# Odd blocks of routed rows transposed by VectorE from quarter-row gathers, even ones by TensorE, and gate and up weights loaded in 8 KB pieces

## What is computed

```python
def body(acc, blk):
    toks, bw, e = blk                      # 128 rows of the table, their weights, one expert
    xb = hp[toks]                          # gather
    yb = (jax.nn.silu(xb @ w_gate[e]) * (xb @ w_up[e])) @ w_down[e]
    return acc.at[toks].add(yb.astype(f32) * bw[:, None]), None
```

## Time and profile before

| | |
|---|---|
| median of three runs | 2494.95 us |
| profiled execution | 2485.66 us |
| its span, first to last instruction | 2483.8 us |
| granted TensorE clock, mean over the span | 0.985 |
| TensorE busy | 2382.5 us (96%) |
| VectorE busy | 1575.5 us (63%) |
| ScalarE busy | 1161.9 us (47%) |
| GpSimd busy | 767.3 us (31%) |
| HBM traffic over the span | 211 GB/s |

### The profile page before, as it was taken

The page is one execution under the profiler, slowest core; times in us unless marked ns, Lnnn a source line. Parts: engine busy times, 40 slices in busy tenths (PEclk is TensorE's granted clock), DMA queues, the critical chain, the costliest instruction groups (busy, mean ns, idle before and its releaser), DMA issues. The chain is left out here.

```text
span 2483.8 us, 49979 instructions
## 1 busy us (share of the span) xinstructions
PE 2382.5 (96%) x11840; PEld 1954.7 (79%) x11842; DVE 1575.5 (63%) x2285; ACT 1161.9 (47%) x1621; POOL 767.3 (31%) x829
## 2 busy tenths in 40 slices
PE   8899999989997799999999999999999999999986
PEld 6677777678886688888888888888888888888875
DVE  6686867768878756555665555656665556655447
ACT  4525253542225645445554445545554445544334
POOL 0010100011110134334543433534443334444327
PEclk9999999989998899999999999999999999999998
DMA  7242323364445579778988878888888789987863
GB/s 254 77 144 98 111 94 111 117 218 164 171 164 206 196 230 284 223 219 270 273 259 233 254 218 263 268 266 262 257 253 243 224 223 274 283 247 222 216 221 136
DMA packets 253808, 524.34 MB, mean 211 GB/s; under 512 B 18065, under 2 KB 165169, under 8 KB 249649
## 3 DMA queue, kind: packets, MB, share of 16 engines
q1 hardware_dynamic: 204464, 336.64, 39.7%
q0 software_dynamic: 48672, 186.86, 29.4%
q10 hardware_dynamic: 608, 0.02, 0.0%
HBM read 386.61 MB, written 136.87 MB: 211 GB/s over the span
## 5 line engine op out<-in xcount | busy, mean ns | idle before, releaser
L2503 PE MATMUL psG<-gu_split,xT_hi 128*128 x2624 | 624.3, 390 | 2.9 <-ACT xT_hi L2340 1.5
L2503 PEld LDWEIGHTS psG<-gu_split,xT_hi 128*128 128x128 f32 x2624 | 493.8, 188 | 106.2 <-issue 3.6
L2326 POOL DMA_INDIRECT acc<-y,si x162 | 290.1, 1791 | 728.6 <-DMA acc<-y,si 413.3
L2409 DVE TENSOR_TENSOR gu_split<-raw_gu,gu_split (+1 forms) x127 | 290.6, 2288 | 175.3 <-ACT gu_split L2344 171.7
L2514 PE MATMUL psG<-gu_split,xT_lo 128*128 x1304 | 339.3, 402 | 5.9 <-issue 5.8
L2514 PEld LDWEIGHTS psG<-gu_split,xT_lo 128*128 128x128 f32 x1304 | 233.1, 188 | 50.1 <-issue 8.7
L2344 ACT ACTIVATE gu_split<-raw_gu x126 | 234.3, 1907 | 33.5 <-issue 33.5
L2301 POOL DMA_INDIRECT xg<-htab,gi x164 | 205.0, 1250 | 130.4 <-POOL gi L2298 109.7
L2409 DVE TENSOR_TENSOR d_lo<-raw_d,d_hi (+1 forms) x64 | 146.7, 2292 | 149.5 <-ACT d_hi L2344 149.5
L2389 ACT ACTIVATE HT_hi<-psH 128x256 fp32r<-128x256 f32 x162 | 62.4, 385 | 351.6 <-PE psH L2521 351.6
L2406 DVE TENSOR_TENSOR xT_lo<-psX,xT_hi 128x512 fp32r<-128x512 f32 x328 | 209.7, 680 | 8.5 <-ACT xT_hi L2340 8.5
(11 more groups left out here) (388 smaller groups left out, 3723.7 us busy)
## 6 DMA issues: line engine op xcount, KB each, us to landing
raw_gu<-in_w_gate_dram SPq DMA_DIRECT2D x64, 1024.0 KB, 6.0
raw_gu<-in_w_up_dram SPq DMA_DIRECT2D x64, 1024.0 KB
raw_d<-in_w_down_dram SPq DMA_DIRECT2D x64, 1024.0 KB, 6.9
wring<-split_d SPq DMA_DIRECT2D x24, 1024.0 KB, 4.8
split_d<-wring POOLq DMA_DIRECT2D x8, 1024.0 KB, 4.2
raw_d<-mixed SPq DMA_DIRECT2D x16, 512.0 KB, 3.9
xt<-in_x_dram SPq DMA_DIRECT2D x16, 512.0 KB, 4.3
htab<-h SPq DMA_DIRECT2D x16, 512.0 KB, 2.6
```

Source lines behind the costliest of these rows:

```text
L2326: nc.gpsimd.indirect_dma_start(out=acc, out_offset=bass.IndirectOffsetOnAxis(ap=si[k][:, 0:1], axis=0), in_=y[k][:], in_offset=None, compu ...
L2409: nc.vector.tensor_tensor(dst, src, hi, ALU.subtract).then_inc(dlo_s if n == 2 else gulo_s, 1)
L2503: nc.tensor.matmul(psG[slot][:], xT_hi[slot][:, c, :], right[:, bass.ds(w, 1), c, :].rearrange("p a n -> p (a n)"), start=(n == 0 and c == ...
```

## The change

A second DRAM table `hcut` holds each token's row in four quarters, each of 256 features and 16 expert weights (1088 bytes). `output_and_route` stores each tile there too (`store_h`: one more DMA of 512 KB per tile; `store_weights`: one more DMA per tile in pieces of 64 bytes), and the zero rows get four more DMAs. `indices()` gains 16 small VectorE operations that write `pidx`, the quarter-row numbers of odd blocks.

In the loop, an odd block is gathered by four indirect DMAs of 128 quarter rows each, so that partition group a (32 partitions) holds quarter a of all 128 rows. VectorE turns it with its 32x32 block transpose: one operation over 1024 elements per partition into `xF`, and one over 128 for the weights. TensorE then only transposes the 128x128 piece with the weights into `psW`. ScalarE and VectorE form `xT_hi` and `xT_lo` of an odd block in one operation each, from SBUF. Even blocks are still transposed by TensorE, now reading every eighth feature.

Gate and up weights land with partition p holding rows 8p to 8p+7, contiguous, 8 KB each, gate and up apart; the split pieces are gate and up in place of the two halves of k. Every eighth feature of a row is the order that goes with it. The index copies `gi` and `si` of the loop move from GpSimd to ScalarE.

```diff
+def gather_pieces(nc, hcut, to, at, done):
+    for g in range(QUADS):
+        nc.gpsimd.indirect_dma_start(out=to[:, g, 0:PIECE], out_offset=None, in_=hcut.rearrange("r a w -> (r a) w"),
+                                     in_offset=bass.IndirectOffsetOnAxis(ap=at[:, g:g + 1], axis=0)).then_inc(done, 16)
...
+                dve.wait_ge(idx_s, 2)
+                odd = idx[:].rearrange("p (b k) -> p b k", k=2)[:, :, 1]
+                for a in range(QUADS):
+                    for g in range(QUADS):
+                        last = nc.vector.tensor_scalar(pidx[a * QP:(a + 1) * QP, :, g], odd[g * QP:(g + 1) * QP], float(QUADS), float(a),
+                                                       ALU.mult, ALU.add)
...
+def runs_view(raw_gu):
+    return raw_gu[:].rearrange("p s k n -> p s (k n)").rearrange("p s (h k n) -> p s h k n", h=2, n=FE)
...
-                        sp.dma_start(dst, w[0, bass.ds(e, 1)].rearrange("a (k p) n -> p (a k) n", p=P)).then_inc(sm, 16)
+                        rows = "a (k p) n -> p (a k) n" if sm is down_in else "a (p k) n -> p (a k) n"
...
 GpSimd, body of the loop
-                    pool.wait_ge(turned[1], s.n + 3)
-                    pool.wait_ge(pairw_s, s.n + 3)
+                    pool.wait_ge(next_gi_s, s.n + 1)
+                    if k == 0:
+                        pool.wait_ge(pairw_s[0], s.turn + 2)
                     carry_wait(pool, passed)
-                    gather(s.n + AHEAD, k, s.n + AHEAD + 1)
-                    nc.gpsimd.tensor_copy(si[k][:], idx[:, bass.ds(s.n, 1)]).then_inc(si_s, 1)
+                    if k:
+                        gather_pieces(nc, hcut, xg[1], gi[1], x_in[1])
+                    else:
+                        gather_rows(nc, htab, xg[0], gi[0], x_in[0])
...
 ScalarE, body of the loop
-                    evac_x(s.n + 3, k)
+                    high_x(s.turn + 2, k)
+                    gather_index(s, k)
                     silu(s.n + 2, 1 - k, s.n + 1)
                     when_first(act, nexts[n + 1], lambda: split_gate_up(nexts[n + 1], s.n + 2))
                     s.wait(act, yps_s[0])
-                    act.wait_ge(added[k], s.turn * 16)
+                    scatter_index(s, k)
...
 VectorE
+            def turn_x(nth):
+                dve.wait_ge(x_in[1], nth * 16 * QUADS)
...
+                nc.vector.transpose(xF[:, 0:KC, :].rearrange("p c (g j) -> p c g j", g=QUADS),
+                                    xg[1][:, :, 0:FEATS].rearrange("p g (i c) -> p c g i", c=KC))
+                nc.vector.transpose(xF[:, KC, :].rearrange("p (g j) -> p g j", g=QUADS),
+                                    xg[1][:, :, FEATS:WIDE]).then_inc(odd_turned, 1)
...
+                    low_x(s.turn + 2, k)
                     s.wait(dve, H_s)
-                    pair_weight(nexts[n + 1], k, s.turn + 2)
-                    product(s.n + 2, 1 - k)
+                    if k == 0:
+                        pair_weight(nexts[n + 1], s.turn + 2, 0)
+                        pair_weight(nexts[n], s.turn + 1, 1)
+                    product(s.n + 2, 1 - k, s.turn + 1 + k)
+                    if k == 0:
+                        turn_x(s.turn + 2)
...
 TensorE
+                rows = xg[0][:, 0:D].rearrange("p (q c) -> p c q", c=KC)
...
+                        m = nc.tensor.transpose(psX[h][:, c, :], rows[:, h * HALF + c], ident[:])
...
-                    pe.wait_ge(x_in[1 - k], (s.turn + k + 2) * 16 )
-                    carry_wait(pe, passed)
-                    for h in range(2):
-                        pe.wait_ge(xlo_s[h], s.n + 3)
-                        turn_x(1 - k, h)
+                    if k:
+                        turn_weights(s.turn + 2)
+                        turn_x(s.turn + 3)
```

More of the change, by code:

```diff
@@ L2128, in _, with load_expert, experts @@
                     down(n)
-def load_expert(eng, w_gate, w_up, w_down, expert, slot, wgu, wd, loaded):
-    for w, sm, dst in zip((w_gate, w_up, w_down), loaded, (wgu[:, slot, :, 0:FE], wgu[:, slot, :, FE:], wd[:, slot])):
-        eng.dma_start(dst, w[0, expert].rearrange("(k p) n -> p k n", p=P)).then_inc(sm, 16)
-def experts(nc, passed, w_gate, w_up, w_down, ident, htab, acc, table, n_turns, idx, xg, gi, gi_s, x_in, acc_out, gu, guhi_s, gulo_s, wgu, wd, loaded, y, si, added,
+def load_expert(eng, w_gate, w_up, w_down, expert, slot, wgu, wd, loaded, by_run=False):
+    gate, up = (runs_view(wgu)[:, slot, h] for h in range(2)) if by_run else (wgu[:, slot, :, 0:FE], wgu[:, slot, :, FE:])
+    for w, sm, dst in zip((w_gate, w_up, w_down), loaded, (gate, up, wd[:, slot])):
+        rows = "(p k) n -> p k n" if by_run and w is not w_down else "(k p) n -> p k n"
+        eng.dma_start(dst, w[0, expert].rearrange(rows, p=P)).then_inc(sm, 16)
+def experts(nc, passed, w_gate, w_up, w_down, ident, htab, hcut, acc, table, n_turns, idx, pidx, tails_s, xg, gi, gi_s, x_in, acc_out, gu, guhi_s, gulo_s, wgu, wd, loaded, y, si, added,
             prefetch_shared, prefetch_hT):
@@ L2175, in experts @@
         xlo_s = [sem(f"xlo_s{i}") for i in range(2)]
-        pairw_s = sem("pairw_s")
+        odd_turned = sem("odd_turned")
+        odd_wturn = sem("odd_wturn")
+        odd_xhi = sem("odd_xhi")
+        odd_xlo = sem("odd_xlo")
+        next_gi_s = sem("next_gi_s")
+        pairw_s = [sem(f"pairw_s{i}") for i in range(2)]
         dhi_s = sem("dhi_s")
@@ L2206, in expert, with column @@
                 return within(self.word & (EXPERTS - 1), 0, EXPERTS - 1)
+            def column(self):
+                share = EXPERTS // QUADS
+                return within((self.word & (EXPERTS - 1)) + (self.word & (EXPERTS - share)), 0, P - 1)
             def next(self):
@@ L2446, in _ @@
             split_first(1)
[L2447 to L2448 removed]
+            low_x(1, 0)
             split_first(2)
[L2450 to L2451 removed]
+            for k in range(2):
+                dve.wait_ge(acc_out[k], 16 * EARLY // 2)
+            pair_weight(block0, 1, 0)
+            dve.wait_ge(tails_s, 1)
+            turn_x(1)
             when_first(dve, block0, lambda: split(block0, 0))
[L2453 to L2455 removed]
+            product(1, 0, 1)
+            low_x(1, 1)
             when_first(dve, block0, lambda: split(block0, 1))
@@ L2483, in _, with turn_x, turn_weights, gate_up_high @@
         def _(pe):
-            def turn_x(slot, half):
-                for c in range(HALF):
-                    m = nc.tensor.transpose(psX[half][:, c, :], xg[slot][:, (half * HALF + c) * P:(half * HALF + c + 1) * P], ident[:])
-                m.then_inc(turned[half], 1)
-            def gate_up_high(nth, slot, entry):
-                for h in range(2):
-                    pe.wait_ge(xhi_s[h], nth)
+            def turn_x(nth):
+                pe.wait_ge(x_in[0], nth * 16)
+                carry_wait(pe, passed)
+                rows = xg[0][:, 0:D].rearrange("p (q c) -> p c q", c=KC)
+                for h in range(2):
+                    if not (isinstance(nth, int) and nth == 1):
+                        pe.wait_ge(xlo_s[h], nth - 1)
+                    for c in range(HALF):
+                        m = nc.tensor.transpose(psX[h][:, c, :], rows[:, h * HALF + c], ident[:])
+                    m.then_inc(turned[h], 1)
+            def turn_weights(nth):
+                pe.wait_ge(odd_turned, nth)
+                if not (isinstance(nth, int) and nth == 1):
+                    pe.wait_ge(pairw_s[1], nth - 1)
+                carry_wait(pe, passed)
+                nc.tensor.transpose(psW[:], xF[:, KC, :], ident[:]).then_inc(odd_wturn, 1)
+            def gate_up_high(nth, slot, entry, seen):
+                if slot:
+                    pe.wait_ge(odd_xhi, seen)
+                else:
+                    for h in range(2):
+                        pe.wait_ge(xhi_s[h], seen)
                 pe.wait_ge(gulo_s, entry.rank() * 2)
```

222 lines of the change are left out of this document (133 added, 89 removed).

## The result

| | kernel before | changed kernel |
|---|---|---|
| median of 4 runs (lowest to highest) | 2493.94 us (2487.02 to 2497.22) | 2585.59 us (2582.45 to 2592.4) |
| ratio, 95% interval | 1 | 1.0375 [1.0343, 1.0407] |
| profiled execution: span, mean granted clock | 2483.8 us, 0.985 | 2585.9 us, 0.965 |

The account below looks back on a forecast made before the run. TensorE was taken to bound the loop; -64.8 + 12 + 0 + 8 + 3 = -42 us from 2494.95 gave 2453 us, 1.7% faster. Range 2436 to 2500; forecast as it stands 2435 to 2468, chance 0.57.

Parts of the forecast that it names:

- Quarter gathers: GpSimd's four gather issues per odd block: just covered by a scatter's landing, 8 us slower in all, bounds 0 and 48.
- scatters and gathers become the bound: Rival in the loop: the chain of scatters sets the pace, 2465 to 2495 us, likeliest 2480; chance 0.20.
- Transposes off TensorE: 82 odd blocks lose TensorE's transposes of x: 64.8 us less, with 12 us back for the weights' transposes, bounds 9 and 22.
- Strided reads on TensorE: TensorE's even-block transposes load every eighth float: taken as zero, bounds 0 and 66 us.
- the rival of 66 us: Strided reads double the pace of TensorE's transposes on even blocks: 66 us more, 2519 us; chance 0.18 including milder cases.
- On VectorE: VectorE's strided transpose of an odd block: 1.3 us plus 0.25 for the weights, bounds 1.2 and 2.7.
- VectorE gets the transposes: VectorE's odd-block transposes fit an idle gap of 2.77 us and cost nothing if the quarter rows come in time.
- Weights in 8 KB pieces: Gate and up weight loads in larger pieces: nothing directly, queues lighter, the scatters' landing taken as unchanged.
- Edges: Before the loop, storing the second table and 16 operations in `indices()`: 3 us more together, bounds 0 and 7.

Follow-up runs that it names:

- no_two_inputs: Changed kernel with VectorE's gate and up weight splits in the loop replaced by one-operand transposes of about equal length: 2497.41 us, ratio 1.002.
- one_gather: Changed kernel with an odd block fetched by one indirect DMA of whole rows instead of four of quarter rows, same bytes: 2494.43 us, ratio 1.0016.
- two_gathers: Changed kernel with an odd block fetched by two indirect DMAs of half rows instead of four of quarter rows, same bytes: 2496.03 us, ratio 1.0026.
- gain_alone: Kernel before with six of TensorE's eight transposes of an odd block left out, nothing else touched: 2462.48 us, ratio 0.9886.
- gain_one_input: Kernel before without six of eight transposes of an odd block, and gate and up splits replaced by one-operand turns of the same length: 2428.27 us.
- weights_only: Kernel before with only the 8 KB gate and up weights and TensorE's transposes of all blocks reading every eighth float: 2498.86 us, ratio 1.0059.
- dense_turn: Changed kernel with VectorE's transpose of an odd block reading neighbouring floats instead of every eighth: 2560.75 us, ratio 1.0281.
- late_turn: Changed kernel with VectorE's two transposes moved to the end of the even iteration, behind its weight splits and the copy of y: 2600.57 us, ratio 1.044.
- early_gather: Changed kernel with the next odd block's four gathers issued in the even iteration, ahead of that iteration's scatter: 2622.15 us, ratio 1.0538.
- before_four: Kernel before with each of VectorE's weight splits in the loop made as four subtractions, all its work kept: 2483.49 us, ratio 0.9981.

## Why the prediction was wrong, step by step

- **Quarter gathers**, the step that failed. It set four issues at 1.0 us against "a scatter's wait for landing", "just" covered, and bounded what is late at 48 us. The cover was counted without VectorE, and without the 0.30 us that stand before each issue: 1.6 + 4 x 1.0 + 5 x 0.30 is 7.1 us from one scatter to the next, not 5.6. The landing took 6.1 us at least, and 0.8 more passed until the next scatter began, 6.9 in all. So where data lands fast, four issues fill the cover even when nothing holds them, and each one held shows. One row quoted ahead of the prediction had the missing term: the third scatter of the earlier trace rows, at 1329.02, lasts 2.69 us where the others last 1.6. It was used only for its start. The first split of the same iteration is in the earlier trace rows; the second ran to 1330.23, and the scatter, which ends at 1331.71, ends 1.48 us after it. The means had it too: 1783 and 1241 ns for 1.6 and 1.0, and "mean 1.24" stands in the prediction without a question why. no_two_inputs measures the term at 88 us for the gate and up splits alone. one_gather and two_gathers keep the splits and come to 2494 and 2496 us. So taking away either the issues or the blocking gives back about 90 us: the term lies in the two together. The row of the second split:

```profile
1327.95 2.28 DVE L2409 TENSOR_TENSOR gu_split<-raw_gu,gu_split  x1
```

- **The rival "scatters and gathers become the bound"** had the right place and the wrong size. It stopped at 2495, because it took the issues as fixed; with them blocked the period rose to 9.88 us, not 9.18. Its premise, that the gain meets the chain, is right by itself: gain_alone gives 27 of 53 us. But that, too, was the blocking: without it (gain_one_input) all of it shows.
- **Transposes off TensorE**, 64.8 us: right in size. In gain_one_input the spared time shows in full.
- **Strided reads on TensorE**: taken as 0, measured 4 us by the steps' starts, 9 for weights_only as a whole; the rival of 66 us fell. The reason given for the zero was misread: 0.8 ns a column is the pace of the transposes, while a load of 140 ns for 128 columns takes 1.1. That the zero came out nearly right is luck as far as that reason goes. **On VectorE** 2.14 us where 1.3 was taken and 2.7 was the bound. It costs 25 us in dense_turn, which "so they cost nothing" had denied. On VectorE the rule of the Trainium skill weighed in the prediction ("SBUF — State Buffer", "Door 1: The DMA port swizzle") agrees with the trace, 2.15 for 1.24 us; on TensorE it shows in the load (193 for 140 ns) and hardly in the pace.
- **VectorE gets the transposes**: its late queue was the named risk, and TensorE's waits for `y` and `HT_lo` are as described. They come mostly from the issues: with one gather the time is back at 2494 us although the transposes stay. Moving the transposes (late_turn) or the gathers (early_gather) only made it worse.
- **Weights in 8 KB pieces**: taken as 0, cost about 13 to 15 us where the chain sets the pace.
- **Edges**: 3 taken, bounds 0 and 7. The loop begins at 861.8 us on the mean of 14 profiles with the second table, 855.8 of 6 without: 6 us.
- **The clock** had no term. one_gather's TensorE, with the same matmuls and a granted clock of 1.00, is busy 775.68 of 800 us for 86 scatters, 9.02 us a block; here it is 9.24, and 162 x 0.22 = 36 us. That they come from TensorE's pauses shows in the trace: from 1000 to 2400 us the clock falls to 1.2 GHz 17 times, each time behind a wait of 2.5 to 3.6 us for `y`.

What stays open: without the blocking of gate and up splits the change is still at 2497, not 2453. The strided read on VectorE (19 to 25 us), the 8 KB pieces (15), the edges (3 more) and the 88 issues that `xT_lo` of odd blocks and `d_lo` still hold would about fill that, but they were not all removed in one run, and the last was not measured by itself.

## What to carry to other kernels

Before work is added to GpSimd's queue, compare the longest issue of each kind with the shortest, and look which VectorE instruction ends at a constant time before the long ones end: here a subtraction with two operands in SBUF. Look for this also where the change moves an operand from PSUM to SBUF. Where an engine's idle time is meant to hide new work, ask what can stretch that work, not only how long it is. And where a wait disappears but the time doesn't (early_gather, late_turn), something else holds the time, and the edit has only moved it.

## What the runs showed of the hardware

- An indirect DMA's issue on GpSimd that begins during a VectorE subtraction of two SBUF operands stands until that ends, and then takes 0.82 to 0.88 us more (gather, usually 0.95 to 1.0) or 1.48 (scatter, usually 1.6). In the changed kernel this holds for 114 of 117. A VectorE transpose of one operand and equal length holds up none of 128 (no_two_inputs), a subtraction with one operand in PSUM none of 29 (changed kernel). The Trainium skill, "SBUF — State Buffer", section "Who interferes with whom", says that such an instruction contends with a GpSimd instruction that reads SBUF, and that the later of the two blocks fully. The traces agree, with 2.69 us for 1.6; a scatter that began 0.16 us before `xT_lo`'s subtraction of an odd block, whose two operands are in SBUF too, kept its 1.59 us. The same section also reports that a `tensor_tensor` did not stall a DMA in an earlier probe, and infers that making descriptors needs the other interface. Here indirect DMAs are stalled by it, 2586 us for 2497, and the measurement decides.
- GpSimd gets in between four subtractions of 0.68 us: in the loop, scatters over 1.75 us and gathers over 1.25 us fall from 28 and 23 to 7 and 3 (before_four).
- The price of issues in a row is a threshold in this loop: 2494, 2496 and 2586 us for one, two and four.
- In the changed kernel the granted clock falls from 2.4 to 1.2 GHz behind TensorE's waits of 2.5 to 3.6 us for `y`, 17 times of 17 between 1000 and 2400 us.
- VectorE's transpose of 128x1024 takes 1.24 us from neighbouring floats, 2.15 from every eighth.
- Eight short VectorE instructions instead of four cost 159 us in the kernel before, with VectorE waiting for nothing the profile names. The cause is open.
